# Three moves on VectorE in the second block: a top-64 choice, the gate logits and one sum of squares

## The reference, cut to what matters

```python
h = rmsnorm(x, norm_mix)
proj = h @ w_in
(qa, ka, va, qi, ki, wi, qb, kb, vb, gdown, ogate) = jnp.split(proj, offsets, axis=-1)
o_a = dsa_mixer(...)      # attention over the 64 keys of highest index score
log_a = jax.nn.log_sigmoid(gdown @ w_gate_up + b_gate) / 16
o_b = gla_mixer(...)      # linear attention in 4 chunks of 64 tokens, one state
o_b = rmsnorm(o_b, gla_norm) * silu(ogate)
x = x + jnp.concatenate([o_a, o_b], axis=-1) @ w_out
x = x + (silu(h2 @ w_ffn_gate) * (h2 @ w_ffn_up)) @ w_ffn_down    # h2 = rmsnorm(x)
```

## Time and profile before

| | us |
|---|---|
| median of 3 runs | 1452.31 (1451.35 to 1452.70) |
| the profiled execution, its own time | 1449.92 |
| its span, first to last instruction | 1448.0 |
| PE busy in the span | 1097.4 |
| DVE / ACT / POOL busy | 354.8 / 306.0 / 311.6 |
| mean granted TensorE clock | 0.880 |

### The profile page before, as it was taken

One profiled execution on the slowest core, in us unless ns is written; L12 is line 12 of the kernel. 1 busy time (PEld: TensorE's weight loads), 2 busy tenths in 40 slices (PEclk: granted clock), 3 DMA queues, 4 the chain that ended last, 5 costly groups with the idle time before them and its releaser, 6 DMA issues.

```text
span 1448.0 us, 19616 instructions
## 1 busy us (share of the span) xinstructions
PE 1097.4 (76%) x8327; PEld 628.8 (43%) x8327; DVE 354.8 (25%) x721; ACT 306.0 (21%) x458; POOL 311.6 (22%) x216
## 2 busy tenths in 40 slices
PE   6999995756756766655666676566658999999997
PEld 6998731311311211211121131121116988999996
DVE  5486520100100001000010010000105745453432
ACT  5753300000000000000000000000006535454442
POOL 6896000000000000000000000000005765385660
PEclk9999997878788777888896887888889999999999
DMA  9510999999999999999999999999999631565530
GB/s 288 175 36 3 411 416 428 426 428 428 429 428 428 429 429 429 429 428 428 429 429 430 428 428 428 430 429 429 427 427 278 185 129 61 196 225 175 181 140 30
DMA packets 95000, 478.06 MB, mean 330 GB/s; under 512 B 11066, under 2 KB 64185, under 8 KB 70361
## 3 DMA queue, kind: packets, MB, share of 16 engines
q1 hardware_dynamic: 94064, 475.76, 81.5%
q10 hardware_dynamic: 873, 1.39, 0.3%
HBM read 475.88 MB, written 1.25 MB: 329 GB/s over the span
## 4 chain that ended last, share of the span: by engine, by line
DMA 57%; PE 36%; DVE 2%; POOL 2%; issue 1%; ACT 1%; ACTq 0%; SPq 0%; DVEq 0%; POOLq 0%
DMA ring<-in_expert_w_down 20%; DMA ring<-in_expert_w_gate 19%; PE bank L1280 18%; DMA ring<-in_expert_w_up 17%; PE bank L2066 4%; PE bank L997 4%; PE bank L1015 2%; POOL slot_r L1254 1%; PE bank L409 1%; PE bank L426 1%; PE bank L422 1%; PE bank L1449 0%; PE bank L1467 0%; DMA vrow<-in_conv_w 0%; PE bank L441 0%
## 5 line engine op out<-in xcount | busy, mean ns | idle before, releaser
L997 PE MATMUL bank<-ring,work 128*32 128x512 f32 x2032 | 314.3, 752 | 209.1 <-DMA ring<-in_expert_w_up 125.4
L997 PEld LDWEIGHTS bank<-ring,work 128*32 128x32 f32 x2032 | 61.6, 124 | 452.4 <-DMA ring<-in_expert_w_up 207.6
L1254 POOL TENSOR_TENSOR slot_r<-ring,slot_r 128x512 fp32r<-128x512 f32 (+1 forms) x123 | 229.2, 1891 | 105.4 <-ACT slot_r L1226 105.3
L1263 POOL TENSOR_TENSOR slot_r<-ring,slot_r 128x512 fp32r<-128x512 f32 x16 | 21.5, 1367 | 965.9 <-ACT slot_r L1232 965.9
L1015 PE MATMUL bank<-ring,work 128*32 128x512 f32 x1024 | 160.8, 765 | 84.5 <-DMA ring<-in_expert_w_down 81.7
L1280 PE MATMUL bank<-slot_r 128*128 128x256 f32 (+2 forms) x1080 | 161.5, 290 | 7.8 <-DVE chan L2385 4.9
L1280 PEld LDWEIGHTS bank<-slot_r 128*128 128x128 f32 (+1 forms) x1080 | 146.3, 194 | 11.5 <-DVE chan L2385 5.2
L1064 DVE TENSOR_TENSOR work<-work,bank 128x512 f32<-128x512 f32 x16 | 11.0, 687 | 497.1 <-PE bank L997 497.1
L1280 PE MATMUL bank<-work_r,slot_r 128*128 128x256 f32 x704 | 126.6, 281 | 0.7 <-DVE chan_r L1788 0.7
L1226 ACT ACTIVATE slot_r<-ring 128x2048 fp32r<-128x2048 f32 x62 | 116.6, 1903 | 2.5 <-DMA ring<-in_w_in 2.5
L1015 PEld LDWEIGHTS bank<-ring,work 128*32 128x32 f32 x1024 | 32.3, 126 | 194.4 <-DMA ring<-in_expert_w_down 122.2
(11 more groups left out here) (400 smaller groups left out, 1027.5 us busy)
## 6 DMA issues: line engine op xcount, KB each, us to landing
ring<-in_expert_w_up SPq DMA_DIRECT2D x64, 2048.0 KB, 35.8
ring<-in_expert_w_down SPq DMA_DIRECT2D x64, 2048.0 KB, 35.9
ring<-in_expert_w_gate SPq DMA_DIRECT2D x63, 2048.0 KB, 35.8
ring<-in_w_in SPq DMA_DIRECT2D x23, 1024.0 KB, 8.1
ring<-in_w_ffn_gate SPq DMA_DIRECT2D x11, 1024.0 KB, 6.2
ring<-in_w_ffn_up SPq DMA_DIRECT2D x11, 1024.0 KB, 5.3
ring<-in_w_ffn_down SPq DMA_DIRECT2D x11, 1024.0 KB, 5.0
ring<-in_w_out SPq DMA_DIRECT2D x8, 1024.0 KB, 5.1
```

What stands on the lines that cost most here:

```text
L997: ins = pe.matmul(bank[b][32 * j:32 * j + 32, :], xg[:, 2 * s + kk, a * CAP:(a + 1) * CAP], w_[:, kk * FF + j * W5:kk * FF + (j + 1) * W5] ...
L1254: ins = eng.tensor_tensor(ring_r[s][:, a:a + step], ring[:, s, a:a + step], ring_r[s][:, a + UNIT:a + UNIT + step].bitcast(F32), ALU.subtract)
L1263: ins = eng.tensor_tensor(ring_r[s][:, at:at + q], ring[:, s, at:at + q], ring_r[s][:, at + UNIT:at + UNIT + q].bitcast(F32), ALU.subtract)
```

## The change: what it does

There are three moves; what is computed stays the same.

1. The sum of squares of tile 1 of `hres` leaves ScalarE (L1603, with t = 1). VectorE takes it with one multiply-and-add instruction of 128 x 1024 elements behind the product of tile 1. Both now stand ahead of `kgw_lo`, which was ahead of the product before.
2. The three gate logit instructions and `sp_sub` move from behind VectorE's halves of units 3, 4 and 5 to ahead of them.
3. `choose(0)` is cut into rounds 0 to 2, 3 to 5, and 6 and 7 with the mask, one group behind each of the three updates of the linear attention's state. It is gone from ahead of `shifted(0)`.

```diff
--- before.py
+++ after.py
@@ -1597,14 +1597,9 @@
             for i in range(4):
                 split_high_part(act, SECOND_FIRST, i)
 
-            def squares_of(t):
-                act.wait_ge(S.scat_added, 4 * E - 2 + 2 * t)
-                act.wait_ge(S.root_ready, ROOT["h2"] + t)
-                act.activation(squares2, hres[:, t], ACT.Square, accum_out=ss[:, t:t + 1]).then_inc(S.root_ready, 1)
-
-            squares_of(0)
+            act.wait_ge(S.scat_added, 4 * E - 2)
+            act.activation(squares2, hres[:, 0], ACT.Square, accum_out=ss[:, 0:1]).then_inc(S.root_ready, 1)
             upper_parts(act, "x2", "norm_mix_2", X2B, xh2)
-            squares_of(1)
             split_high(act, SECOND_FIRST + 1)
             act.wait_ge(slot_in[7], landed(7, "second", 3))
             act.activation(kgw_hi, kgw_w, ACT.Copy).then_inc(S.act_chain, 1)
@@ -1793,11 +1788,13 @@
         def second_dve(dve, link):
 
             lower_parts(dve, "x2", "norm_mix_2", X2B, xh2, xl2)
-            dve.wait_ge(S.act_chain, 4)
-            dve.tensor_tensor(kgw_lo, kgw_w, kgw_hi.bitcast(F32), ALU.subtract).then_inc(S.chan_ready, 1)
             dve.wait_ge(S.small_in, 48)
             dve.wait_ge(S.scat_added, 4 * E)
             dve.tensor_tensor(tokm[:, 1], hres[:, 1], nf_bc, ALU.mult).then_inc(S.sumsq_ready, 1)
+            dve.tensor_tensor_reduce(work0[:, 0:D], hres[:, 1], hres[:, 1], 1.0, 0.0, ALU.mult, ALU.add, ss[:, 1:2])\
+                .then_inc(S.root_ready, 1)
+            dve.wait_ge(S.act_chain, 4)
+            dve.tensor_tensor(kgw_lo, kgw_w, kgw_hi.bitcast(F32), ALU.subtract).then_inc(S.chan_ready, 1)
             dve.wait_ge(S.root_ready, ROOT["h2"] + 2)
             dve.tensor_scalar(floor2, ss, EPS / D, EPS * EPS, ALU.mult, ALU.add).then_inc(S.sumsq_ready, 1)
             split_low(dve, SECOND_FIRST + 1, True)
@@ -1819,6 +1816,10 @@
             dve.tensor_tensor(kgw, bank[0][0:KGW, 0:T], rs2_bc[0:KGW], ALU.mult).then_inc(S.rows2_evac, 1)
             split_low(dve, SECOND_FIRST + 2, True)
             scaled(3, qbT, 6, float(B_DK) ** -0.5)
+            dve.wait_ge(S.loga_out, 1)
+            link(dve.tensor_tensor(logaT, bank[3][:, :].rearrange("p (j t) -> p j t", j=2), bc(vec("b_gate_2", 0, 2), [P, 2, T]), ALU.add))
+            link(dve.tensor_scalar(bcum, logaT, -1.0, None, ALU.mult))
+            dve.tensor_tensor(bcum, bcum, logaT, ALU.min).then_inc(S.sp_sub, 1)
             for n in range(3, SB_SLOTS):
                 split_low(dve, SECOND_FIRST + n, True)
 
@@ -1839,18 +1840,17 @@
                     ins.then_inc(S.relu_used, 1)
                     dve.wait_ge(S.relu_used, first + i + 1)
 
-            def choose(t):
+            def choose(t, first=0, last=TOPK // 8):
+
                 sc, ns = score[t], NS[t]
-                link(dve.memset(sc[0:CHUNK, ns - CHUNK:ns], NEG))
-                for n in range(TOPK // 8):
+                if first == 0:
+                    link(dve.memset(sc[0:CHUNK, ns - CHUNK:ns], NEG))
+                for n in range(first, last):
                     link(dve.max(top8, sc))
                     link(dve.match_replace(sc, top8, sc, TAKEN))
-                dve.tensor_scalar(addm[t], sc, TAKEN, NEG, ALU.not_equal, ALU.mult).then_inc(S.mask_ready, 1)
-
-            dve.wait_ge(S.loga_out, 1)
-            link(dve.tensor_tensor(logaT, bank[3][:, :].rearrange("p (j t) -> p j t", j=2), bc(vec("b_gate_2", 0, 2), [P, 2, T]), ALU.add))
-            link(dve.tensor_scalar(bcum, logaT, -1.0, None, ALU.mult))
-            dve.tensor_tensor(bcum, bcum, logaT, ALU.min).then_inc(S.sp_sub, 1)
+                if last == TOPK // 8:
+                    dve.tensor_scalar(addm[t], sc, TAKEN, NEG, ALU.not_equal, ALU.mult).then_inc(S.mask_ready, 1)
+
             dve.wait_ge(S.sp_ln, 1)
             link(dve.scalar_tensor_tensor(logaT, logaT, 0.0, bcum, ALU.min, ALU.subtract))
             link(dve.tensor_scalar(logaT, logaT, 1.0 / GATE_NORM, None, ALU.mult))
@@ -1889,6 +1889,7 @@
                         ins = dve.scalar_tensor_tensor(st, st, eb[r, j, CHUNK * n + CHUNK - 1:CHUNK * n + CHUNK],
                                                        bank[7][r, j * T + b * P:j * T + (b + 1) * P], ALU.mult, ALU.add)
                 ins.then_inc(S.st_ready, 1)
+                choose(0, 3 * n, min(3 * n + 3, TOPK // 8))
             for t in range(TT):
                 dve.wait_ge(S.ob_copied, t + 1)
                 squares = work(t)
@@ -1907,7 +1908,6 @@
                 dve.wait_ge(S.logit2_ready, u + 1)
                 dve.tensor_scalar(m, m, -1.0, None, ALU.mult).then_inc(S.nmax_ready, 1)
 
-            choose(0)
             shifted(0)
             shifted(1)
             dve.wait_ge(S.proj2_evac, 5)
```

## The result

The changed kernel takes 1444.07 us (median), the kernel before 1451.53 in the runs beside it: ratio 0.9949, 95% interval 0.9938 to 0.996. One of the six runs of the changed kernel took 3341.62 us, and why stays open; the ratio leaves it out, and the median of the other five is 1443.86. The profiled execution took 1443.36 us, its span 1441.5.

A forecast was written before the change was run, and what follows sets the result against it. The prediction took PE to bound block two, with DMA bounding the untouched experts' stage of block one. Terms +0.4 - 1.55 - 0.23 - 2.30 - 1.5 = -5.2 us, from 1452.31 to 1447.1 us; range 1444.9 to 1449.8.

The forecast's parts named there:

- The bound and the method: Block two: PE's list bounds it, and time won before 1200 us stays won if the other engines keep up.
- Part 1: Start of block two: the `rms_ready` wait of 1.08 us goes, PE waits 1.4 us for `kgw_lo` instead; +0.4 us.
- rival A: Same place as part 1: VectorE keeps its turn for all three, `kgw_lo` in time, -1.08 for +0.4; 1445.6 us, chance 0.16.
- Part 2: Gate logits before `both(3)`: PE's wait for `sp_sub` goes, -1.55 us, and the later wait for L1750, -0.23 us.
- Part 3: Before `both(11)`: rounds fall into VectorE's idle time at no cost, and PE's wait for `shifted(0)` goes, -2.30 us.
- rival D: State updates: rounds take turns with GpSimd's splits, 3.25 us each, so `gla_step(3)` is 4.4 us late; 1453.0 us, chance 0.04.
- The clock: At `both(11)`: without the idle time ahead of it PE runs at full clock, 6.0 us instead of 7.52; -1.5 us.
- The range: Whole kernel: 1444.9 to 1449.8 us, taking in the forecast, A and its bound, B, C and E.

The follow-up runs named there:

- `plain_square`: The changed kernel with tile 1's sum of squares as a plain product that leaves no sum; rows(0) to rows(1) took 9.20 us, no whole time given.
- part 2 alone: The kernel before with only the three gate logit lines moved ahead of VectorE's halves; ratio 0.9987 (0.9976 to 0.9999), block two 3.34 us less.

## Why the prediction was wrong

**The bound and the method: right.** PE's list bounds block two, time taken off it stays off it, and behind `both(12)` every stage kept its length to 0.1 us.

**Part 1: the failed step.** The prediction had "GpSimd's first split has its turn to 1107.1; the new sum to 1108.2", from the one exchange of turns in the earlier trace rows. The runs showed the sum ahead of the split, so `kgw_lo` was there at 1108.6 instead of 1109.9. The part gained 1.16 us instead of losing 0.4. That is half of rival A, held at 0.16: VectorE kept its turn for product and sum, but one split got in ahead of `kgw_lo`, an order that the prediction did not price. It gave slightly more than A's bound of 1.08, since the stretch from the first matmul of L1489 to rows(1) also fell from 0.47 to 0.36 us. Where all three went ahead (`plain_square`), `kgw_lo` was in time and the stage took 9.20 us, 1.34 less. The remark against A, that GpSimd took its turn at once in the earlier trace rows, was the error: its request had there stood 0.51 us before the end of VectorE's instruction, here 0.32.

**Part 2: right.** -1.62 and -0.29 for -1.55 and -0.23. The halves were quicker than priced, which nobody on PE needed.

**Part 3: the mechanism right, one term short.** The price of 2.30 was the wait of `qk_(2)` alone. A second wait, of `qk_(3)` for `shifted(1)`, is not in PE's list but among its weight loads; timeline of the kernel before, 1192 to 1194 us:

```profile
1193.18 0.29 PEld L1449 LDWEIGHTS bank<-early 64*128 64x128 f32 x2 [0.29 <-DVE cols L1905]
```

So the four matmuls of L1449 in the earlier trace rows took 1.28 us; they take 0.70 when `shifted(1)` is out. The step said that the maximum of unit 1 would be in time, and did not subtract what it had cost. The stage gave 2.94, 0.64 more than priced; 0.57 of it lies between the first matmul of L1449 and `both(11)` (1.21 before, 0.64 after). Rounds beside GpSimd cost nothing, as stated; rival D did not happen.

**The clock: right in size, for a narrower reason.** -1.50 for -1.5. The idle time was needed for the fall but did not suffice: with part 2 alone the wait of 2.3 us stayed and the clock did not fall, so there the same reasoning would have been 1.5 us off.

**The range.** It took in A at its forecast bound but nothing for a term counted short in the same direction. The two terms give 1.56 and 0.64 us more than the sum; with block two's 7.45 us off 1452.31 the time would be 1444.86, just below the lower bound of 1444.9. The rest of the 0.8 us is not the change: the kernel before took 1451.53 in the runs beside the changed one, 0.78 less than the 1452.31 from which the forecast counts.

## What to carry to other kernels

Price a wait by the stage around it (start of the group before to start of the group after), not by the longest row of the waits: here a second wait, seen only among the weight loads (PEld), and the group that it stretched hid behind it. Where VectorE and GpSimd meet, give both orders of turns as cases of equal standing unless a row has the same offset between the two requests. Put short work of an engine where it waits for the bounding engine anyway: eight rounds moved there cost nothing and gave 4.4 us.

## What was not expected of the hardware

A fill of 32 elements (0.09 us) between two VectorE instructions let a waiting GpSimd instruction in, and the next one of VectorE took 1.07 us longer. An instruction on two elements took 1.25 us behind a split, 0.16 otherwise. And the clock fell behind 1.4 us of idle time in one kernel and not behind 2.3 us in another, though the kernel before and part 2 alone each gave the same answer in three executions.
